# A new order for the opening of a two-block transformer kernel: x first, all adaLN chunks next, rows in four column groups

## The reference, cut to what matters

```python
def rms_norm(x, g):
    xf = x.astype(jnp.float32)
    y = xf * lax.rsqrt(jnp.mean(xf * xf, axis=-1, keepdims=True) + EPS)
    return (y * g.astype(jnp.float32)).astype(x.dtype)

def adaln_mod(cond, w_mod, b_mod):
    m = jax.nn.silu(cond) @ w_mod + b_mod
    return m.reshape(cond.shape[:-1] + (N_MOD, D_MODEL))

def ffn_sublayer(x, m, i, g, w_in, w_out):
    u = modulate(rms_norm(x, g), m, i)          # x * (1 + scale) + shift
    return x + 0.5 * m[:, 3 * i + 2][:, None] * swiglu(u, w_in, w_out)
```

## Time and profile before

| | us |
|---|---|
| median of three runs | 2852.77 |
| lowest, highest | 2848.59, 2855.56 |
| span of the profiled execution, first to last instruction | 2851.3 |
| PE, DVE, ACT busy in it | 2696.1, 1533.2, 963.0 |

### The profile page before, as it was taken

The page is one execution under the profiler, slowest core; times in us unless marked ns, Lnnn a source line. Parts: engine busy times, 40 slices in busy tenths (PEclk is TensorE's granted clock), DMA queues, the critical chain, the costliest instruction groups (busy, mean ns, idle before and its releaser), DMA issues.

```text
span 2851.3 us, 35137 instructions
## 1 busy us (share of the span) xinstructions
PE 2696.1 (95%) x14390; PEld 2146.0 (75%) x14390; DVE 1533.2 (54%) x2710; ACT 963.0 (34%) x1716; POOL 52.4 (2%) x55
## 2 busy tenths in 40 slices
PE   6999998999999999999999989999999899997796
PEld 3888887876667888887888878798998787784342
DVE  3776754356224777738767444645555665444111
ACT  3322224257113322224222243644444532332111
POOL 0000000000000000000000000000000000000320
PEclk8999999999999999999999999999999899998998
DMA  7344442200223444433466323044544112256997
GB/s 300 140 190 181 182 178 83 96 28 6 99 89 108 167 176 190 172 118 148 164 256 272 149 103 111 23 151 160 185 156 167 60 60 89 89 201 270 405 379 305
DMA packets 56959, 456.54 MB, mean 160 GB/s; under 512 B 10720, under 2 KB 21344, under 8 KB 21856
## 3 DMA queue, kind: packets, MB, share of 16 engines
q1 hardware_dynamic: 49600, 446.01, 40.7%
q0 software_dynamic: 6912, 6.32, 0.7%
q10 hardware_dynamic: 288, 1.97, 0.2%
HBM read 497.25 MB, written 1.05 MB: 175 GB/s over the span
## 4 chain that ended last, share of the span: by engine, by line
PE 85%; DVE 5%; DMA 4%; ACT 3%; issue 1%; SPq 0%; POOL 0%; DVEq 0%; ACTq 0%; POOLq 0%
PE ps L496 59%; PE ps L1236 3%; PE ps L1577 3%; PE ps L2188 2%; PE ps L1228 1%; PE ps L1156 1%; PE ps L1133 1%; PE ps L3168 1%; PE ps L501 1%; PE ps L2795 1%; PE ps L2247 1%; DMA BIG<-eup 1%; DMA U<-edn 1%; DMA U<-eup,extra_ids 1%; PE ps L566 1%
## 5 line engine op out<-in xcount | busy, mean ns | idle before, releaser
L496 PE MATMUL ps<-UL,fh 128*128 128x512 f32 (+1 forms) x1408 | 517.1, 367 | 22.5 <-DVE UL L769 21.7
L496 PE MATMUL ps<-UH,fl 128*128 128x512 f32 (+1 forms) x1408 | 515.3, 366 | 0.0
L496 PE MATMUL ps<-UH,fh 128*128 128x512 f32 (+1 forms) x1408 | 514.7, 366 | 0.0
L490 DVE TENSOR_TENSOR fl<-wr,fh 128x1024 fp32r<-128x1024 f32 (+1 forms) x304 | 328.7, 1081 | 245.4 <-ACT fh L483 244.8
L483 ACT CAST fh<-wr 128x1024 fp32r<-128x1024 f32 (+1 forms) x304 | 282.2, 932 | 199.7 <-PE ps L496 181.4
L496 PEld LDWEIGHTS ps<-UL,fh 128*128 128x128 f32 x1408 | 268.4, 191 | 68.6 <-DVE UL L769 21.4
L542 DVE SCALAR_TENSOR_TENSOR acc<-wr,CA 128x1024 f32<-128x1024 f32 x256 | 312.7, 1222 | 3.7
L496 PEld LDWEIGHTS ps<-UH,fh 128*128 128x128 f32 x1408 | 268.9, 191 | 41.9
L496 PEld LDWEIGHTS ps<-UH,fl 128*128 128x128 f32 x1408 | 268.8, 191 | 41.3
L496 PE MATMUL ps<-HH,fh 128*128 128x512 f32 (+1 forms) x704 | 255.5, 363 | 0.0
L496 PE MATMUL ps<-HL,fh 128*128 128x512 f32 (+1 forms) x704 | 255.5, 363 | 0.0
(11 more groups left out here) (513 smaller groups left out, 4134.2 us busy)
## 6 DMA issues: line engine op xcount, KB each, us to landing
wr<-ws SPq DMA_DIRECT2D x130, 2048.0 KB, 7.8
wr<-ws SPq DMA_DIRECT2D x32, 1408.0 KB, 5.9
wr<-eup SPq DMA_DIRECT2D x32, 1024.0 KB, 11.7
BIG<-eup SPq DMA_DIRECT2D x22, 1024.0 KB, 16.2
wr<-edn SPq DMA_DIRECT2D x16, 1024.0 KB, 14.3
wr<-ws SPq DMA_DIRECT2D x8, 1536.0 KB, 6.4
BIG<-edn SPq DMA_DIRECT2D x11, 1024.0 KB, 11.3
wr<-ws SPq DMA_DIRECT2D x9, 1024.0 KB, 6.3
```

The costliest lines, as they stand in the source:

```text
L490: e.tensor_tensor(lv, raw_tile(sp.units[n]), hv.bitcast(F32), ALU.subtract).then_inc(*low_done.inc("low", event))
L496: i = e.matmul(out, l, r, start=first and n == 0, stop=last and n == len(pairs) - 1, skip_group_check=True)
```

## The change

x is loaded first, then the four chunks in the order 0, 2, 1, 3, and then the first input weights in two loads of 1 MB, one pair each; everything behind them keeps its order. The squares go to eight tiles of their own, and PE sums them by eight full-width matmuls with an all-ones weight, which spreads the sum at once; ACT then makes the inverse root of all 512 positions as exp(-0.5 ln(mean + eps)) with `act_inverse_root` (L695), as the mixers do. Rows of a chunk are made in four column groups of 32, with two blocks each, from a copy of the conditions padded with zeros to 32 columns (SCP); one DVE copy of 128 partitions takes them out, and the selecting matrix adds four groups. All chunk work stands ahead of the first product; the FFN's first loop holds products only. ACT and DVE have a written order of their own for the first norm (`act_first_norm`, `dve_first_norm`; `norm`, `scaled` and `low` in them are the steps of the norm as before). The diff, cut to its core:

```diff
+FIRST_CHUNKS = (0, 2, 1, 3)
...
     for half in range(2):
-        for c in range(6):
-            m = 2 if c < 5 else 1
-            load = ("fin", l, f, half * 11 + 2 * c, m)
+        c = 0
+        for m in (1, 1, 2, 2, 2, 2, 1) if (l, f, half) == (0, 0, 0) else (2, 2, 2, 2, 2, 1):
+            load = ("fin", l, f, half * 11 + c, m)
...
-    out = [("wmodk", 0), ("wmodk", 2)]
+    out = [("wmodk", ch) for ch in FIRST_CHUNKS]
...
-                if (l, f, half, p) == (0, 0, 0, 0):
-                    out.extend([("wmodk", 1), ("wmodk", 3)])
...
+        SCP = BIG[:, 10240:10496].rearrange("p (k c) -> p k c", c=32)
+        first_squares = [BIG[:, 512 * k:512 * k + 512] for k in range(8)]
...
         def pe_mod_rows(e, ch):
...
-            for k in range(4):
-                for g in range(2):
-                    i = e.matmul(b[64 * g:64 * g + 2, :], SC[:, 0:2, 4 * g + k], w[:, 4 * g + k, :], start=k == 0, stop=k == 3,
+            for k in range(2):
+                for g in range(4):
+                    i = e.matmul(b[32 * g:32 * g + 32, :], SCP[:, 2 * g + k, :], w[:, 2 * g + k, :], start=k == 0, stop=k == 1,
...
         def dve_mod_rows(e, ch):
-            b = psum.of("mod cols", ch)
             e.wait_ge(*at("mod sums", ch))
-            for g in range(2):
-                e.tensor_copy(Z[ch][64 * g:64 * g + 2, :], b[64 * g:64 * g + 2, :]).then_inc(*dve.inc())
-            dve.mark("mod rows", ch)
+            e.tensor_copy(Z[ch], psum.of("mod cols", ch)[:, :]).then_inc(*dve.inc("mod rows", ch))
...
         def pe_begin(e):
...
+            for k in range(8):
+                e.wait_ge(*at("square", "load", k))
+                i = e.matmul(NB[:, :], ones, first_squares[k], start=k == 0, stop=k == 7, skip_group_check=True)
+            i.then_inc(*sums.inc("stats", "load"))
+            e.wait_ge(*at("padded"))
             pe_mod_rows(e, 0)
+            pe_mod_rows(e, 2)
             pe_mod_cols(e, 0)
-            pe_stats(e, "load", 512, None)
-            pe_mod_rows(e, 2)
-            pe_spread(e, ("ffn", 0, 0), 4, rinv)
             pe_mod_cols(e, 2)
+            pe_mod_rows(e, 1)
+            pe_mod_cols(e, 1)
+            pe_mod_rows(e, 3)
+            pe_mod_cols(e, 3)
...
         def act_begin(e):
...
+            act_log_exp(e)
             for c, x in cond_rows(0, 0):
                 act_cond_row(e, (0, 0), c, x)
+            e.wait_ge(*at("x"))
             for k in range(8):
-                act_square(e, "load", k, 512)
+                e.activation(first_squares[k], X[:, k, :], ACT.Square).then_inc(*act.inc("square", "load", k))
             e.wait_ge(*at("eps"))
-            act_root_table(e)
-            act_root(e, ("ffn", 0, 0), "load", 512)
+
+        def act_first_norm(e, name, segs, shift, sp):
+            act_inverse_root(e, name, "load", 512)
...
+            e.wait_ge(*at("gains", 0))
+            for k in range(4):
+                norm(k)
+            for _ in range(4):
+                high_parts(e, sp, sp.next_one())
+            e.wait_ge(*at("gains", 1))
+            for k in range(4, 8):
+                norm(k)
+
+        def dve_begin(e):
+            e.memset(eps[:, :], EPS).then_inc(*dve.inc("eps"))
+            e.memset(SCP, 0.0).then_inc(*dve.inc())
+            e.wait_ge(*at("ident"))
+            e.tensor_reduce(sel, ident.rearrange("p (g c) -> p c g", g=4)[:, 0:2, :], AX.X, ALU.add).then_inc(*dve.inc())
+            e.wait_ge(*at("silu c"))
+            e.wait_ge(*dve.now())
+            e.tensor_copy(SCP[:, :, 0:2], SC[:, 0:2, :].rearrange("p c k -> p k c")).then_inc(*dve.inc("padded"))
+
+        def dve_first_norm(e, name, segs, gain, scale, sp):
...
+            dve_mod_rows(e, 0)
+            scaled(0)
+            scaled(1)
+            dve_mod_rows(e, 2)
+            dve_mod_cols(e, 0)
+            scaled(2)
+            dve_mod_cols(e, 2)
+            dve_gains(e, segs, gain, scale, slice(0, 4))
+            dve.mark("gains", 0)
+            scaled(3)
+            dve_mod_rows(e, 1)
+            low(0)
+            dve_mod_cols(e, 1)
+            low(1)
+            low(2)
+            dve_mod_rows(e, 3)
+            scaled(4)
+            low(3)
+            scaled(5)
+            dve_mod_cols(e, 3)
+            dve_gains(e, segs, gain, scale, slice(4, 8))
+            dve.mark("gains", 1)
+            for k in (6, 7, 8, 9):
+                low_parts(e, sp, sp.next_one())
+                if k < 8:
+                    scaled(k)
+            for k in range(4, 8):
+                low(k)
...
         def pe_ffn(e, l, f, prev, segs, nb_free):
...
             for d in range(11):
-                if prev == "load" and d == 2:
-                    pe_mod_rows(e, 1)
-                    pe_mod_cols(e, 1)
-                if prev == "load" and d == 3:
-                    pe_mod_rows(e, 3)
-                if prev == "load" and d == 4:
-                    pe_mod_cols(e, 3)
...
             for n, load in enumerate(loads):
-                if n == 1:
+                if n == 0:
                     e.dma_start(X[:, :, :].rearrange("p a b -> p (a b)"), ws[0:128 * 4096].rearrange("(p w) -> p w", p=128)).then_inc(
```

More of the change, by code:

```diff
@@ L597, in pe_begin @@
                 pe_cond_row(e, (0, 0), c, x)
-            for ch in (0, 2, 1, 3):
+            for ch in FIRST_CHUNKS:
                 mod_banks[ch] = psum.take("mod cols", ch)
+            for k in range(8):
[3 more added lines that the diff above has]
+            e.wait_ge(*at("padded"))
             pe_mod_rows(e, 0)
+            pe_mod_rows(e, 2)
             pe_mod_cols(e, 0)
-            pe_stats(e, "load", 512, None)
-            pe_mod_rows(e, 2)
-            pe_spread(e, ("ffn", 0, 0), 4, rinv)
             pe_mod_cols(e, 2)
[L607 to L621, removed]
+            pe_mod_rows(e, 1)
+            pe_mod_cols(e, 1)
+            pe_mod_rows(e, 3)
+            pe_mod_cols(e, 3)
         def act_begin(e):
@@ L627, in act_begin, with norm @@
             act.mark("silu c")
+            act_log_exp(e)
             for c, x in cond_rows(0, 0):
                 act_cond_row(e, (0, 0), c, x)
+            e.wait_ge(*at("x"))
             for k in range(8):
-                act_square(e, "load", k, 512)
+                e.activation(first_squares[k], X[:, k, :], ACT.Square).then_inc(*act.inc("square", "load", k))
             e.wait_ge(*at("eps"))
-            act_root_table(e)
-            act_root(e, ("ffn", 0, 0), "load", 512)
+        def act_first_norm(e, name, segs, shift, sp):
+            act_inverse_root(e, name, "load", 512)
+            def norm(k):
+                u = u_tiles.of("u", name, k)
+                e.wait_ge(*at("scaled", name, k))
+                for c, (lo, hi) in enumerate(segs):
+                    e.activation(u[:, lo:hi], u[:, lo:hi], ACT.Identity, bias=shift[:, c, k:k + 1],
+                                 scale=AB[:, c, k:k + 1]).then_inc(*act.inc())
+                e.wait_ge(*act.now())
+                e.copy(UH[:, k, :], u[:, :]).then_inc(*act.inc("u high", name, k))
+            e.wait_ge(*at("gains", 0))
[6 more added lines that the diff above has]
+                norm(k)
@@ new lines, in dve_begin, with scaled, low @@
+        def dve_begin(e):
[7 more added lines that the diff above has]
+        def dve_first_norm(e, name, segs, gain, scale, sp):
+            def scaled(k):
+                u, old = u_tiles.take("u", name, k)
+                if old:
+                    e.wait_ge(*at(*old))
+                if k == 0:
+                    e.wait_ge(*at("spread", name))
+                e.tensor_tensor(u[:, :], X[:, k, :], NB[:, :], ALU.mult).then_inc(*dve.inc("scaled", name, k))
+            def low(k):
+                e.wait_ge(*at("u high", name, k))
+                e.tensor_tensor(UL[:, k, :], u_tiles.of("u", name, k)[:, :], UH[:, k, :].bitcast(F32), ALU.subtract).then_inc(
+                    *dve.inc("u", name, k))
+            dve_mod_rows(e, 0)
[26 more added lines that the diff above has]
+                low(k)
@@ L650, in act_square @@
                     e.wait_ge(*at(*old))
[L651 to L654, removed]
+            e.wait_ge(*at("x", prev, k))
             if gain is not None:
@@ L733, in act_norm @@
                 act_inverse_root(e, name, prev, T)
-            elif prev != "load":
+            else:
                 act_root(e, name, prev, T)
@@ L739, in act_norm @@
                 e.wait_ge(*at("scaled", name, k))
-                if prev == "load" and k == 4:
-                    e.wait_ge(*at("late gains"))
                 for c, (lo, hi) in enumerate(segs):
@@ L749, in dve_norm @@
         def dve_norm(e, name, T, segs, gain, scale, split, sp, early):
-            begin = name == ("ffn", 0, 0)
-            dve_gains(e, segs, gain, scale, slice(0, 4) if begin else slice(0, 8))
-            if not begin and name[0] == "ffn":
+            dve_gains(e, segs, gain, scale)
+            if name[0] == "ffn":
                 dve_root(e, name, T)
```

(23 more changed lines are left out.)

3 lines of the change are left out of this document (2 added, 1 removed).

## The result

The changed kernel takes 2821.03 us (median of four runs, 2819.23 to 2824.72) against 2850.82 us before (2848.59 to 2855.56): 29.8 us less, ratio 0.990 with a 95% interval of 0.9885 to 0.9914. The forecast was 2824.8, or 28 us less.

A forecast was written before the change was run, and what follows sets the result against it. TensorE holds 85% of the span, so time is won only at the start: product 31 moves from 71.7 to 43.8 us, 27.9 less. Span 2851.3 becomes 2823.4, plus 1.5 gives 2824.8 us; range 2817 to 2836.

The forecast's parts named there:

- product 31: First product behind the opening 30 in the first loop: begins at 37.0 + 6.8 = 43.8 us, against 71.7 before.
- warm-up: First products at L496: some 5.8 us at half clock, costing 2.7 us, the same before and after, so it cancels.
- Statistics on PE: Sum of squares for the first norm: sixteen ones-matmul records take 6.9 us plus 0.17, from 11.7 to 18.7 us.
- Rows in four groups: Chunk rows on PE: four records at once, 1.9 us a chunk instead of 3.60, 1.7 less.
- rival B: Chunk rows: four groups run two at a time, rows 3.6 us, first product 40.3, gain 24, about 2828 us; chance 0.07.
- Transfers: Opening loads, 4.9 us per 2 MB: x 10.8, chunks 0, 2, 1, 3 at 15.6, 20.5, 25.4, 30.2, weights 32.7 and 35.1.
- rival E: Opening loads: x and four chunks share the queue, all land near 30 us; gain 13, 2840 us; chance 0.02.
- New order: Chunk steps ahead of products: first gains at 25.1 us, chunk 3's rows 30.2 to 32.1, first product taken at 37.0.
- the other end: Chunk 3's rows at half clock: rows 1.8 us longer, less what DVE's queue covers, products start at 38.1 us.
- Rival A: Chunk work at half clock from the first ones-matmul: first product 47 us, gain 17.9, 2834.9 us; chance 0.10.
- Nothing gives it back: After product 31: all later waits are relative to product progress, so the 27.9 us won at the start stay won.
- Rivals C and D: C: DVE behind early products gives all back, 2850 us, chance 0.03. D: long half clock from 37 us, slower, chance 0.02.

The follow-up runs named there:

- second and third profile: The changed kernel unaltered, run and profiled twice more: medians 2823.80 and 2820.97 us, ratios 0.9912 and 0.9901 to the kernel before.
- the run with the weights third: Changed kernel with first input weights loaded behind chunks 0 and 2, ahead of 1 and 3, as before: 2825.62 us, ratio 0.9921 to the kernel before.
- the overlapped version: Changed kernel, weights loaded third, first-loop products of steps 0 to 2 ahead of and between chunk 1 and 3 steps, ACT/DVE reordered: 2822.90 us, ratio 0.9907.

## Why the prediction was right

**Direction and size.** By its own steps the forecast put product 31 at 43.8 and a warm-up of 2.7 us on top; with 66 products more, product 97 at 61.4. Measured: 63.46, 61.51 and 59.75. The gain of 27.9 us stands between the 26.2, 28.1 and 29.9 of the three openings against the one profile of before. The whole time fell by 29.8 us where the first opening accounts for 26.2; the rest is the spread of the later part. So that the total came within 2 us of the forecast is in part luck: the ratios measured with the second and third profile are worth 25.1 and 28.2 us.

**Statistics on PE**: 6.9 + 0.17 us from 11.7 to 18.7 forecast, 7.13 from 11.71 to 18.84 measured. Right.

**Rows in four groups**: 1.9 us forecast, 1.93 measured at the full clock, 3.62 for two chunks. The upper bound of 3.6 (rival B) is excluded, and so is the estimate of 2.3 us from the ratio in "TensorE: Matmul & The Clock Gate" (Measured speedup vs the span model) of the Trainium skill. The run with two groups shows that the 1.7 us a chunk are needed in the chunks ahead of the last too, which the forecast did not ask.

**Transfers**: chunk 2 at 20.3 and chunk 1 at 25.2 against 20.5 and 25.4, which also excludes rival E. Chunk 3 landed at 31.45 in the first profile where 30.2 was forecast, and at 30.60 and 30.23 in the two others. The even spacing of 4.9 us holds for four transfers; the fifth came up to 1.4 us late. The trace of before showed this already: its fifth large load, chunk 1, was issued at 3.55 and landed 28.5 us later, at 32.0, 6.6 us after the fourth. The forecast took the spacing of the first ones for all. The run with the weights third confirms that the arrival of chunks 1 and 3 binds the changed order; in the second and third profile of the change chunk 3's rows started 0.35 and 0.17 us after the landing, held by the steps of chunk 1.

**New order**: gains at 25.1 forecast, ready at 24.8 (24.66 + 0.17); first product 37.0 forecast, 39.60, 36.93 and 36.40 measured. The step that was off in the first profile is the clock: full clock from 11.7 to 24.7 held, and lasted until 30 us, but chunk 3's rows ran at half, 3.64 instead of 1.9, and the turn too. The forecast had it as the other end, with a start at 38.1; it left out that the turn gets slower as well (0.8 us) and added it to no late landing (1.4 us). In the two other profiles the half clock fell on chunk 1's rows, which the forecast had not considered; they had room for most of it. Rival A put the fall too early: between 12 and 25 us the grant was 1.00 in all three.

**Warm-up**: in the first profile 4.3 us of half clock under the products instead of 5.8, 0.7 us less lost; in the others 5.8 and 3.2.

**"Nothing gives it back"** held: 26.2 us at product 97, 26.2 at product 1501. Rivals C and D (VectorE behind the first loop, a long half clock) have nothing in the trace: PE is 100% busy from 40 us to 200, where the chain ends that I read, and at the full clock from 44.

**What the forecast did not say** is which part brings it. The steps out of the product stream alone bring 14.0 us at product 97, 9.7 (6.3 to 13.1) in the whole time. The remaining 12 to 16 us at product 97 come from the rest together: undone one at a time on the changed kernel, the load order costs 4 to 8 us, two column groups 3 to 6 and x second 2 to 6, each range from the first and the best profile of the change. One load for the weights lies 1 to 5 us behind, but its timeline puts this down to a late landing and the clock. Each of these is one profile against a spread of 3.7 us, so only the load order is clear of it by size; for the others the evidence is in their chains. They don't add up to the rest, since each undone part takes over the chain from the others. The wide statistics and the halves of the weights' load have no number of their own.

## What to carry to other kernels

Before an opening is reordered, write down for every item when it arrives and when the engine has finished the item before; only the later of the two can be improved, and the same new load order was worth 4 us or more in one version and nothing in the other. Short steps between products are not harmful in themselves: with nothing queued behind them the overlapped version starts its products 9 to 12 us earlier and reaches product 97 (60.90) within the change's own spread. A gap in TensorE's work can cost twice: behind the 2.6 us before chunk 3's rows the grant was 0.50 until 43.9, behind the 1.1 us before chunk 1's rows until 29.1 in the second profile. So look at the granted clock of the stretch after each gap.

## What the runs showed that I had not expected

Matmuls whose result nobody reads keep the clock: ten of them (20 records, 0.23 us each) held the grant at 1.00 from 24 to 56 us, where it was 0.50 from 31 to 43 in the first profile without them. The clock and the landings together make the opening of one and the same kernel move by 3.7 us: the clock is half for chunk 3's rows in one profile (3.64 us), for chunk 1's in two (3.58 and 3.19 us), and chunk 3's landing moves by 1.2 us. And five transfers of 2 MB from one queue, all issued by 4 us, don't land evenly: in eight of the fourteen profiles one of the 2 MB loads that land before 37 us took 6.0 to 6.6 us, the others 4.7 to 5.1. It was the fifth load in five of them, the fourth in the run with the weights in one load (20.01 to 26.41), and a later one in two overlapped runs. In the first profile of the change 360 to 483 GB/s moved in each microsecond from 8 to 42 us all the same; what the time goes to is not shown.
